# The sample's share of the input projections in float32, two column halves side by side

## The chip, the core and the metric

The kernel runs on one core of one Trainium2 chip. The metric is the device time of one execution in microseconds. Of the kernel before there are three timed runs, and one execution was taken by the hardware profiler.

## What is computed

The reference runs two layers of an encoder for 256 prompt tokens (two tiles of 128) and 64 sample tokens (one tile), with shared weights. All arrays are float32. The part that matters here is the token mixing between the two feed-forward halves:

```python
def _token_mix(h, pos, lambda_init, w_in, w_out, g_qk, w_lambda, g_sub, kv_past, s0):
    rq, rk, rv, rg, dq, dk, dv = jnp.split(h @ w_in, split_points, axis=-1)   # w_in: 1024 x 3072
    rq, rk = rotary of both, rk scaled
    o_r, s_new = _retention(rq, rk, rv, s0)
    o_r = _rms_norm(o_r) * jax.nn.silu(rg)
    dq, dk = rotary of _rms_norm of both
    o_d = _diff_attention(dq, k_all, v_all, lam, pos, k_pos)      # sample: 512 cached keys + its own 64
    o_d = _rms_norm(o_d, g_sub) * (1.0 - lambda_init)
    mix = jnp.concatenate([o_r, o_d], axis=-1) @ w_out
    return mix, dk, dv, s_new
```

Each layer computes `h` by an RMS norm with a scale and a shift for each of the two request groups, and writes the new keys, values and retention states out.

## The kernel before

**Precision.** A product of float32 tensors is made of three matmuls in the type that the listing calls F32R: both operands are split into a high part (`w_hi`, `h_hi`, by ScalarE, `split` and `norm_heads`) and a rest (`w_lo`, `h_lo`, by VectorE), and TensorE (PE in the rows) adds hi x hi, hi x lo and lo x hi. A matmul on plain float32 operands leaves two records in the trace, one for each of its passes.

**The projections.** `in_step` (L718 on) has 12 steps a layer. A step is 512 columns of `w_in` and half of the contraction, four blocks of 128 called k; two steps (kh 0 and 1) make one column block cb of 512: DK, DQ, DVAL, RQK, RV, RG. For each k the tokens are the stationary operand (two tiles of 128, one of 64) and 512 weight columns stream past: 9 matmuls of 512 columns (L740, L741, L745), three of them for the sample's 64 tokens. Outputs go to PSUM banks 0 to 2 (3 to 5 for DQ).

**The order on TensorE** is written out by hand. `attention_at(l, q)` puts the attention's pieces between the k blocks; q counts them, 48 a layer, four a step. q 10, 12, 14, 16 turn the four tiles of the key cache (`turn_nth`, L697, which waits on `cache_landed`), q 17 to 26 turn keys and queries, q 24 to 46 hold scores, transposed probabilities and weighted values of the five attention units, q 44 and 47 the retention scores. Behind the last step stand `mix_turn`, `retention` and `out_half`.

**Weights.** Each step's 1 MB lands in `raw[s % 2]` by two DMAs that SyncE's queue (SP in the rows) issues in program order (`load`, L458). Before the load of step s may start, VectorE must have finished the split of step s - 2, since that is the last reader of the buffer. The split of step s is made while step s - 1 runs. `load_in(l, 2)`, `load_in(l, 3)`, the key cache (L526) and then `load_in(l, 4)` follow one another in the queue.

**What follows the projections.** ScalarE copies (`copy_out`) or squares the tiles, VectorE rotates (`rope`, `rope_ret`), GpSimd makes the powers (`power`) and stores keys and values. All operations on the sample's tile have 64 partitions and 512 elements. VectorE's order around the wait at q 37 is: `maxima(2)`, a split, `combine(2)`, `rope_ret(0)`, `diff_sums(0)`, `rope_ret(1)`, a split, `diff_scale(0)`; `weigh(2)` at q 37 waits for the last of them. ScalarE's `exps(3)` stands behind the copies of the turns of q 38 and q 39 in its order, and `turn_probs(3)` at q 40 waits for what VectorE makes of it (`combine(3)`).

Of the kernel before, what the change touches and what calls it, by code (L numbers as in the profile page):

```python
# [19 lines left out]
F32 = mybir.dt.float32  # L20
# [21 lines left out]
ROWS = [P, P, DEC]  # L42
TILE0 = [0, P, SEQ]
# [75 lines left out]
def shape_tables():  # L119
# [9 lines left out]
    for tile in range(3):  # L129
        pos = (np.arange(P) + (PAST if tile == 2 else tile * P)).astype(np.float32)  # L130
# [6 lines left out]
        for part, f in enumerate((1.0, DH ** -0.5)):  # L137
            o = 128 * tile + 64 * part
            t[:, T_RC + o:T_RC + o + 64] = c * f
            t[:, T_RS + o:T_RS + o + 64] = s * f  # L140
    j, i = np.arange(P)[:, None], np.arange(256)[None, :]
    for h in range(HEADS):
# [4 lines left out]
        for tile in range(3):  # L147
            last = SEQ - 1 - tile * P if tile < 2 else DEC - 1
            t[:, T_KDEC + 4 * tile + h] = np.exp(g[h] * (last - np.arange(P))) if tile < 2 else \
                np.where(np.arange(P) < DEC, np.exp(g[h] * (last - np.minimum(np.arange(P), DEC - 1))), 0)  # L150
# [12 lines left out]
def encoder(nc, x_prompt, x_sample, cache_k, cache_v, state_ret, c_prompt, c_sample, w_ada, b_ada, g_norm,  # L163
# [17 lines left out]
    with ExitStack() as ctx:  # L181
# [49 lines left out]
        gsub_rows = nc.alloc_sbuf_tensor_at("gsub_rows", [P, P], F32, offset=at_rows + 3072)  # L231
        first_raw = [nc.alloc_sbuf_tensor_at(f"first_raw{s}", [P, 1024], F32, offset=at + 12288 + 4096 * s)
# [91 lines left out]
        rqk_copied = sem("rqk_copied")  # L324
        ret_first = sem("ret_first")
# [65 lines left out]

        def mix_blocks(m):
            t = MIX_ORDER[m][0]
            if MIX_ORDER[m] != (2, 1):
                return ps[:, MIX_BANK[m], :].rearrange("p (b r) -> p b r", b=4)[:, :, 0:ROWS[t]]
            return ps[:, MIX_BANK[m], 0:4 * DEC].rearrange("p (b r) -> p b r", b=4)
# [40 lines left out]
        def _(sp):  # L437
# [10 lines left out]
            def load(l, s, j, parts):  # L448
# [7 lines left out]
                wait_apart(sp, lo_ready, 4 * nn + 2 * (s % 2) + 2)  # L456
                for dst, src in parts:
# [85 lines left out]
        def _(pe):  # L543
# [146 lines left out]
            def turn(l, n, src, rows):  # L690
# [5 lines left out]
                for b in range(4):  # L696
                    mm = pe.transpose(ps[:, turn_bank(n), b * P:b * P + rows], src[0:rows, b * P:(b + 1) * P],  # L697
                                      ident[0:rows, 0:rows])
# [16 lines left out]

            def in_step(l, i, between):
# [7 lines left out]
                for hf in range(2):  # L724
                    for kk in range(2):
                        between(4 * i + 2 * hf + kk)
                        if kk == 0:
                            half_ready(l, s, 0, hf)
# [3 lines left out]
                        outs = [(ps[0:ROWS[t], first + t, :], slice(TILE0[t], TILE0[t] + ROWS[t])) for t in range(3)]  # L732
                        if cb == 0:
                            pe.wait_ge(hh_ready, l * 3 * KB + KB + k + 1)
                        for t, (out, tok) in enumerate(outs):
                            if k == 0 and cb == 4:
                                wait_apart(pe, rqk_copied, l * 3 + t + 1)
                            elif k == 0 and cb in (3, 5):
                                wait_apart(pe, copied, l * 9 + (0 if cb == 3 else 3) + t + 1)
                            pe.matmul(out, h_hi[:, k, tok], wh, start=(k == 0), stop=False)  # L740
                            pe.matmul(out, h_hi[:, k, tok], wl, start=False, stop=False)  # L741
                        if cb == 0:
                            pe.wait_ge(hl_ready, l * 3 * KB + KB + k + 1)
                        for out, tok in outs:
                            mm = pe.matmul(out, h_lo[:, k, tok], wh, start=False, stop=(k == KB - 1))  # L745
                mm.then_inc(step_done, 1)

# [52 lines left out]
            def weigh(l, n):  # L800
# [16 lines left out]
                else:  # L817
                    u = n - 2
                    for i in range(5):
                        w, v = (P, cache_val[i]) if i < 4 else (DEC, v_nat[:, 2, :])  # L820
                        for j, h in enumerate(heads):
                            mm = pe.matmul(ps[j * DEC:(j + 1) * DEC, bank, u * DV:(u + 1) * DV],
                                           probs_t[0:w, n % 2, i * P + j * DEC:i * P + (j + 1) * DEC],
                                           v[0:w, h * DV:(h + 1) * DV], start=(i == 0), stop=(i == 4))
# [3 lines left out]
            def ret_scores(l, a):  # L828
# [6 lines left out]
                for o, n, k0, q0, q1 in ((0, P, 0, 0, SEQ), (256, P, P, P, SEQ), (384, DEC, SEQ, SEQ, TOK)):  # L835
                    for b in range(2):
                        rows = slice(b * DH, (b + 1) * DH)
                        mm = pe.matmul(ps[0:n, SCORE_BANK + b, o:o + q1 - q0], rqk_t[rows, 2 + a, k0:k0 + n],
# [3 lines left out]
            def retention(l):  # L842
# [17 lines left out]
                def own(h):  # L860
                    return pe.matmul(ps[0:DEC, 2, h * DV:(h + 1) * DV], sa[0:DEC, h, :], rv_nat[0:DEC, 2, h * DV:(h + 1) * DV],
                                     start=True, stop=False)

                def carried(h):
                    rows = slice(h % 2 * DH, h % 2 * DH + DH)
                    return pe.matmul(ps[0:DEC, 2, h * DV:(h + 1) * DV], q_dec[rows, h // 2, :], state_in[rows, h // 2, :],
                                     start=False, stop=True)
# [977 lines left out]
```

## Time and profile before

| | |
|---|---|
| median of 3 runs | 1453.66 us (1451.62 to 1453.81) |
| the profiled execution, its own time | 1451.63 us |
| its span, first to last instruction | 1449.8 us |
| TensorE busy | 1391.1 us, 96% |
| VectorE, ScalarE, GpSimd busy | 865.4, 572.4, 399.1 us |
| DMA moved | 261.12 MB, mean 180 GB/s |
| the projection steps, layers 0 and 1 | 317.5 to 452.5 us and 1018.1 to 1153 us |

The table is read as follows: TensorE is busy nearly all the time, so most of the span is its stream, and a change to that stream counts unless something else sets the moment at which the stream may go on. In the stages of the projections there are such moments, and the rows below are taken from there. The lines of the page carry sums over the span; the timeline gives the start and length of single instructions, with the idle time before them and its releaser in brackets; the table by stretches gives busy times and the granted TensorE clock (1.00 is 2.4 GHz, 0.50 is 1.2 GHz).

### The profile page before, as it was taken

What the parts mean: (1) busy time and instruction counts of PE and PEld (TensorE: products, weight loads), DVE (VectorE), ACT (ScalarE), POOL (GpSimd) and SP (SyncE); (2) the same over time, 40 slices, a digit from 0 to 9 for tenths busy, and PEclk for the clock granted to TensorE, in tenths of its full rate; (3) what the DMA queues carried; (4) which work ended last, traced back from release to release, by engine and by line L of the source; (5) the groups of instructions that cost most, each with busy time, mean ns of one, the idle gap of its engine ahead of it and who ended that gap; (6) DMA issues with size and microseconds to landing.
All of it is one profiled execution on the core that took longest, in us unless ns stands there. A gap on an engine that the chain in (4) does not pass through costs nothing.

```text
span 1449.8 us, 23657 instructions
## 1 busy us (share of the span) xinstructions
PE 1391.1 (96%) x9537; PEld 1248.1 (86%) x9537; DVE 865.4 (60%) x1390; ACT 572.4 (39%) x972; POOL 399.1 (28%) x284
## 2 busy tenths in 40 slices
PE   4999999999989999999999999999999889999998
PEld 2899999977767999999999998999676679999997
DVE  2466555557565765556656665564776567666752
ACT  3343334234434543435334343433443544444421
POOL 1133233412101233333423323342120023333422
PEclk8899999999999999999999999999999999999999
DMA  9777787725321587776558777674442128455751
GB/s 318 249 241 244 228 265 219 225 81 194 125 68 52 159 254 225 239 224 193 145 151 255 241 225 232 191 206 156 149 152 89 59 86 257 130 146 147 188 157 40
DMA packets 322749, 261.12 MB, mean 180 GB/s; under 512 B 8193, under 2 KB 288337, under 8 KB 322513
## 3 DMA queue, kind: packets, MB, share of 16 engines
q1 hardware_dynamic: 321248, 255.15, 57.3%
q0 software_dynamic: 1392, 4.46, 0.9%
q8 instruction: 76, 1.25, 0.4%
q14 instruction: 33, 0.26, 0.1%
HBM read 255.12 MB, written 4.46 MB: 179 GB/s over the span
## 4 chain that ended last, share of the span: by engine, by line
PE 90%; DVE 4%; SPq 2%; ACT 1%; issue 1%; DVEq 1%; DMA 1%; ACTq 0%; POOL 0%
PE ps L573 23%; PE ps L575 22%; PE ps L574 22%; PE ps L740 4%; PE ps L599 4%; PE ps L741 4%; PE ps L745 4%; DVE w_lo L1282 1%; SPq L479 1%; SPq L458 1%; PE ps L697 1%; PE ps L652 1%; PE ps L651 1%; PE ps L656 1%; PE ps L765 1%
## 5 line engine op out<-in xcount | busy, mean ns | idle before, releaser
L1282 DVE TENSOR_TENSOR w_lo<-raw,w_hi 128x1024 fp32r<-128x1024 f32 (+3 forms) x304 | 475.3, 1605 | 68.7 <-ACT w_hi L1012 67.4
L573 PE MATMUL ps<-h_hi,w_hi 128*128 128x322 f32 x1344 | 423.2, 315 | 0.0
L575 PE MATMUL ps<-h_hi,w_lo 128*128 128x322 f32 x1344 | 417.6, 311 | 0.0
L574 PE MATMUL ps<-h_lo,w_hi 128*128 128x322 f32 x1344 | 416.6, 310 | 0.0
L1012 ACT ACTIVATE w_hi<-raw 128x1024 fp32r<-128x1024 f32 (+1 forms) x304 | 324.1, 1114 | 224.7 <-PE ps L575 184.4
L1751 POOL TENSOR_TENSOR w_lo<-raw,w_hi 128x512 fp32r<-128x512 f32 (+1 forms) x112 | 209.2, 1868 | 643.3 <-ACT w_hi L1012 643.3
L573 PEld LDWEIGHTS ps<-h_hi,w_hi 128*128 128x128 f32 x1344 | 253.2, 188 | 24.0 <-issue 24.0
L574 PEld LDWEIGHTS ps<-h_lo,w_hi 128*128 128x128 f32 x1344 | 254.3, 189 | 0.0
L575 PEld LDWEIGHTS ps<-h_hi,w_lo 128*128 128x128 f32 x1344 | 252.6, 188 | 0.0
L1077 ACT ACTIVATE t_buf<-t_buf,shift_w 128x256 f32<-128x256 f32 (+1 forms) x176 | 65.9, 421 | 415.1 <-DVE t_buf L1356 415.1
L573 PE MATMUL ps<-g_hi,w_hi 128*128 128x320 f32 x704 | 218.0, 310 | 0.0
L575 PE MATMUL ps<-g_hi,w_lo 128*128 128x320 f32 x704 | 217.4, 309 | 0.0
L574 PE MATMUL ps<-g_lo,w_hi 128*128 128x320 f32 x704 | 217.4, 309 | 0.0
L1355 DVE COPY shift_w<-ps 128x4 f32<-128x4 f32 x88 | 14.2, 161 | 202.0 <-PE ps L575 194.2
L573 PEld LDWEIGHTS ps<-g_hi,w_hi 128*128 128x128 f32 x704 | 132.4, 188 | 1.3 <-issue 1.3
L574 PEld LDWEIGHTS ps<-g_lo,w_hi 128*128 128x128 f32 x704 | 132.4, 188 | 0.0
L575 PEld LDWEIGHTS ps<-g_hi,w_lo 128*128 128x128 f32 x704 | 132.4, 188 | 0.0
L740 PE MATMUL ps<-w_hi,h_hi 128*128 128x512 f32 (+1 forms) x288 | 122.0, 424 | 6.9 <-ACT h_hi L1051 6.9
L741 PE MATMUL ps<-w_lo,h_hi 128*128 128x512 f32 (+1 forms) x288 | 116.7, 405 | 0.0
L1756 POOL TENSOR_TENSOR g_lo<-f_buf,g_hi 128x320 fp32r<-128x320 f32 x88 | 113.6, 1291 | 0.0
L1788 POOL TENSOR_TENSOR small<-small,minus_half 128x8 f32<-128x8 f32 (+4 forms) x24 | 31.1, 1299 | 283.4 <-DVE small L1442 150.4
L1371 DVE SCALAR_TENSOR_TENSOR x<-ps,mod,x 128x256 f32<-128x256 f32 x96 | 31.6, 377 | 126.5 <-PE ps L575 126.5
(173 smaller groups left out, 1470.9 us busy)
## 6 DMA issues: line engine op xcount, KB each, us to landing
raw<-in_w_ff_up SPq DMA_DIRECT2D x176, 512.0 KB, 5.1
ada_raw<-in_w_ada SPq DMA_DIRECT2D x134, 512.0 KB, 6.6
raw<-in_w_ff_down SPq DMA_DIRECT2D x64, 704.0 KB, 6.3
raw<-in_w_in SPq DMA_DIRECT2D x48, 512.0 KB, 4.8
raw<-in_w_out SPq DMA_DIRECT2D x16, 512.0 KB, 3.9
first_raw<-in_w_ada SPq DMA_DIRECT2D x10, 512.0 KB, 8.2
out<-arena POOLq DMA_DIRECT2D x9, 256.0 KB, 3.3
arena<-in_cache_k SPq DMA_DIRECT2D x2, 1024.0 KB, 7.3
```

Source lines behind the costliest of these rows:

```text
L573: pe.matmul(out, hi, mhi, start=start, stop=False)
L574: pe.matmul(out, hi, mlo, start=False, stop=False)
L575: return pe.matmul(out, lo, mhi, start=False, stop=stop)
L599: mm = pe.matmul(ps[32 * j:32 * j + 2, 4 + group % 2, 0:256], groups_c[:, :, k], ada_slot(n)[:, 256 * j:256 * j + 256], start=(k == 0), st ...
L740: pe.matmul(out, h_hi[:, k, tok], wh, start=(k == 0), stop=False)
L741: pe.matmul(out, h_hi[:, k, tok], wl, start=False, stop=False)
L745: mm = pe.matmul(out, h_lo[:, k, tok], wh, start=False, stop=(k == KB - 1))
L1012: act.activation(w_hi[s % 2][:, hf * w:(hf + 1) * w], raw[s % 2][:, hf * w:(hf + 1) * w], ACT.Copy).then_inc(hi_ready, 1)
L1077: last = act.activation(t_buf[:, s % 2, a:b], t_buf[:, s % 2, a:b], ACT.Silu, bias=shift_w[:, s % 2, 0, g:g + 1])
L1282: dve.tensor_tensor(w_lo[s % 2][:, cols], raw[s % 2][:, cols], w_hi[s % 2][:, cols], ALU.subtract)\
L1751: pool.tensor_tensor(w_lo[s % 2][:, cols], raw[s % 2][:, cols], w_hi[s % 2][:, cols], ALU.subtract)\
L1756: pool.tensor_tensor(block_of(g_lo, i + 2 * j), f_buf[:, i % 2, :], block_of(g_hi, i + 2 * j), ALU.subtract)\
```

## The change

The sample's three matmuls for each k are replaced by a float32 product from the landed weights. `in_sample` multiplies `h_sample` (64 tokens, float32, written by ScalarE instead of the sample's columns of `h_hi`) with `raw`: columns 0 to 255 into PSUM partitions 0 to 63, columns 256 to 511 into partitions 64 to 127. The call stands ahead of the step's own matmuls, behind them for cb 0. The sample's tensors behind the projections then have 128 partitions and 256 columns (`COLS`), heads 0 and 1 in the lower half, 2 and 3 in the upper; copies, squares, rotations, powers, turns, retention and stores follow that. A load must now wait until `in_sample` of the step two before has read the buffer (`sample_done`). `copy_out` takes the sample first. In `retention` the sample's matmuls have a new order with one self-wait for three. The sample's keys and values go out by two DMAs each instead of one.

```diff
@@ load
                 wait_apart(sp, lo_ready, 4 * nn + 2 * (s % 2) + 2)
+                if S_IN + 2 <= s < S_OUT + 2:
+                    wait_apart(sp, sample_done, l * IN + s - 2 - S_IN + 1)
@@ new
+            def in_sample(l, i):
+                s, cb, kh = S_IN + i, i // 2, i % 2
+                nn = l * (STEPS // 2) + s // 2
+                if cb == 0:
+                    wait_apart(pe, hh_ready, l * 3 * KB + KB + 4 * kh + 4)
+                if cb == 4 and kh == 0:
+                    wait_apart(pe, rqk_copied, l * 3 + 1)
+                elif cb in (3, 5) and kh == 0:
+                    wait_apart(pe, copied, l * 9 + (0 if cb == 3 else 3) + 1)
+                wait_apart(pe, raw_landed[s % 2], 32 * nn + 32)
+                for k in range(4):
+                    for a in range(2):
+                        o = k // 2 * W_STD + k % 2 * 512 + 256 * a
+                        mm = pe.matmul(ps[a * DEC:(a + 1) * DEC, 5 if cb == 1 else 2, 0:256], h_sample[:, 4 * kh + k, :],
+                                       raw[s % 2][:, o:o + 256], start=(kh == 0 and k == 0), stop=(kh == 1 and k == 3))
+                mm.then_inc(sample_done, 1)
@@ in_step
                         between(4 * i + 2 * hf + kk)
+                        if cb and hf == 0 and kk == 0:
+                            in_sample(l, i)
...
-                        for t, (out, tok) in enumerate(outs):
+                        for t in range(2):
...
                 mm.then_inc(step_done, 1)
+                if cb == 0:
+                    in_sample(l, i)
@@ retention
-                for h in (0, 2):
-                    own(h)
-                    carried(h)
-                own(1).then_inc(ret_first, 1)
-                wait_apart(pe, ret_first, l * 3 + 1)
-                carried(1).then_inc(ret_first, 1)
-                wait_apart(pe, ret_first, l * 3 + 2)
-                own(3).then_inc(ret_first, 1)
-                wait_apart(pe, ret_first, l * 3 + 3)
-                carried(3).then_inc(ret_done, 1)
+                own(0, True)
+                carried(0, False)
+                own(1, True)
+                sample_state(0)
+                sample_state(1)
+                carried(2, True).then_inc(ret_first, 1)
+                wait_apart(pe, ret_first, l + 1)
+                carried(1, False)
+                own(2, False)
+                own(3, True)
+                carried(3, False).then_inc(ret_done, 1)
+                sample_state(2)
+                sample_state(3)
@@ norm_heads
-                        last = act.activation(h_hi[:, kb, a:b], f_buf[:, kb % 2, a:b], ACT.Identity,
-                                              bias=mod_col(g, 1, 0, kb))
+                        last = act.activation((h_hi[:, kb, 0:SEQ], h_sample[:, kb, :])[g], f_buf[:, kb % 2, a:b],
+                                              ACT.Identity, bias=mod_col(g, 1, 0, kb))
@@ copy_out
-                    act.wait_ge(step_done, l * STEPS + S_IN + i + 3)
-                    for t in range(3):
-                        act.activation(dst[0:ROWS[t], t, :], ps[0:ROWS[t], t, :], func).then_inc(done, 1)
+                    for t in (2, 0, 1):
+                        if t == 2:
+                            act.wait_ge(sample_done, l * IN + i + 1)
+                        elif t == 0:
+                            act.wait_ge(step_done, l * STEPS + S_IN + i + 3)
+                        act.activation(dst[:, t, 0:COLS[t]], ps[:, t, 0:COLS[t]], func).then_inc(done, 1)
```

## Rows read from the trace of the kernel before

**Rows 1.** The page: busy time by engine, share of the span, instructions.
```profile
PE 1391.1 (96%) x9537; PEld 1248.1 (86%) x9537; DVE 865.4 (60%) x1390; ACT 572.4 (39%) x972; POOL 399.1 (28%) x284
```

**Rows 2.** Groups by form: stationary, moving shape, count, busy us, mean ns; first of three.
```profile
L740 PE MATMUL ps<-w_hi,h_hi 128*64 128x512 f32 x96 | 38.9, 405 | 0.0
```

**Rows 3.** Timeline of TensorE, start and length in us: one k block.
```profile
391.21 0.40 PE L740 MATMUL ps<-w_hi,h_hi 128*128 128x512 f32 x1
...
393.32 0.40 PE L740 MATMUL ps<-w_hi,h_hi 128*128 128x512 f32 x1
```

**Rows 4.** Timeline of TensorE: the sample's weighted values (two halves), then whole-array ones.
```profile
431.07 0.85 PE L745 MATMUL ps<-w_hi,h_lo 128*128 128x512 f32 x3
431.86 1.09 PE L822 MATMUL ps<-cache_val,probs_t 128*64 128x128 f32 x16
432.88 0.44 PE L822 MATMUL ps<-arena,probs_t 64*64 64x128 f32 x4
433.25 0.50 PE L740 MATMUL ps<-w_hi,h_hi 128*128 128x512 f32 x1
433.58 0.39 PE L741 MATMUL ps<-w_lo,h_hi 128*128 128x512 f32 x1
...
446.15 1.06 PE L815 MATMUL ps<-arena,probs_t 128*128 128x128 f32 x8
446.96 0.48 PE L740 MATMUL ps<-w_hi,h_hi 128*128 128x512 f32 x1
```

**Rows 5.** Timeline of TensorE: a modulation pair, float32, four side by side.
```profile
66.47 1.05 PE L599 MATMUL ps<-ada_raw,silu_c 128*2 128x256 f32 x16
67.45 0.42 PE L573 MATMUL ps<-h_hi,w_hi 128*128 128x322 f32 x1
```

**Rows 6.** Groups by form, weight loads: the loads of the first block of rows 4.
```profile
L822 PEld LDWEIGHTS ps<-cache_val,probs_t 128*64 128x64 f32 x64 | 3.8, 145 | 5.8 <-issue 5.8
```

**Rows 7.** Timeline of SyncE's queue, layer 0, and the key cache's line: issue to landing.
```profile
323.41 0.88 SPq L458 DMA_DIRECT2D raw<-in_w_in  x2
...
324.41 0.40 SPq L526 DMA_DIRECT2D arena<-in_cache_k  x1
...
DMA to landing us min/median/max: 7.0/7.3/7.6
```

**Rows 8.** Timeline of TensorE, layer 0, steps 0 to 2: q 0, q 8, q 10.
```profile
317.55 0.57 PE L740 MATMUL ps<-w_hi,h_hi 128*128 128x512 f32 x1 [3.46 <-ACT h_hi L1051]
...
336.36 0.40 PE L740 MATMUL ps<-w_hi,h_hi 128*128 128x512 f32 x1
...
340.52 0.60 PE L697 MATMUL ps<-tab,arena 128*128 128x128 f32 x4
```

**Rows 9.** Timeline of TensorE: q 32, then the waits at q 37 and q 40, both layers.
```profile
395.42 0.60 PE L795 MATMUL ps<-tab,arena 128*128 128x128 f32 x4
...
412.89 1.57 PE L822 MATMUL ps<-cache_val,probs_t 128*64 128x128 f32 x16 [2.02 <-DVE arena L1599]
427.82 0.63 PE L795 MATMUL ps<-tab,arena 128*128 128x128 f32 x4 [2.60 <-DVE arena L1643]
1114.73 1.09 PE L822 MATMUL ps<-cache_val,probs_t 128*64 128x128 f32 x16 [2.01 <-DVE arena L1599]
1128.25 0.63 PE L795 MATMUL ps<-tab,arena 128*128 128x128 f32 x4 [2.58 <-DVE arena L1643]
```

**Rows 10.** Table by stretches: busy us by engine, then PEclk, DMA share, GB/s.
```profile
317.50:321.00 3.50, 3.45 (x9) 2.38 (x10) 3.22 (x11) 1.99 (x6) 0.00 (x0) 0.54 0.00 0
415.00:418.00 3.00, 2.84 (x15) 2.04 (x12) 1.87 (x6) 0.00 (x0) 0.00 (x0) 0.50 0.35 121
```

**Rows 11.** Timeline behind step 11: the wait for the gate copies, the sample's retention.
```profile
454.55 1.13 PE L850 MATMUL ps<-arena 128*128 128x128 f32 x8 [1.19 <-issue]
...
457.40 0.43 PE L861 MATMUL ps<-arena 64*64 64x128 f32 x2
...
460.28 0.45 PE L882 MATMUL ps<-arena,k_dec 128*64 128x128 f32 x4
```

More of the change, by code:

```diff
@@ L390, in block_of, with halves, mix_dst @@
             return a[:, i, :] if isinstance(i, int) else a[:, bass.ds(i, 1), :].rearrange("p a b -> p (a b)")
+        def halves(blocks):
+            return blocks[:, :, SEQ:TOK].rearrange("p (a b) r -> p b a r", a=2)
         def mix_blocks(m):
[L393 to L396, printed above, removed]
+            t, half = MIX_ORDER[m]
+            if t < 2:
+                return ps[:, MIX_BANK[m], :].rearrange("p (b r) -> p b r", b=4)
+            if half == 1:
+                return ps[:, MIX_BANK[m], 0:4 * DEC].rearrange("p (b r) -> p b r", b=4)
+            return ps[:, MIX_BANK[m], 0:4 * DEC].rearrange("p (b a r) -> p b a r", b=2, a=2)
+        def mix_dst(m, buf):
+            t, half = MIX_ORDER[m]
+            blocks = buf[:, 4 * half:4 * half + 4, :]
+            return halves(blocks) if (t, half) == (2, 0) else blocks[:, :, TILE0[t]:TILE0[t] + ROWS[t]]
         DIFF_TILES, DIFF_BANK = (1, 2, 0), (6, 6, 7)
@@ L695, in turn @@
                     wait_apart(pe, mod_taken, FFN_GROUPS[l, 0][-1] + 1)
-                for b in range(4):
-                    mm = pe.transpose(ps[:, turn_bank(n), b * P:b * P + rows], src[0:rows, b * P:(b + 1) * P],
-                                      ident[0:rows, 0:rows])
+                for b in range(4 if rows == P else 2):
+                    mm = pe.transpose(ps[:, turn_bank(n), b * P:(b + 1) * P], src[:, b * P:(b + 1) * P], ident)
                 mm.then_inc(turned, 1)
@@ L834, in ret_scores @@
                     wait_apart(pe, ret_decayed, l * 2 + 1)
[L835 removed]
+                for o, keys, k0, q0, q1 in ((0, slice(0, P), 0, 0, SEQ), (256, slice(0, P), P, P, SEQ),
+                                            (384, slice(a * DEC, (a + 1) * DEC), SEQ, SEQ, TOK)):
                     for b in range(2):
                         rows = slice(b * DH, (b + 1) * DH)
[L838 removed]
+                        mm = pe.matmul(ps[keys, SCORE_BANK + b, o:o + q1 - q0],
+                                       rqk_t[rows, 2 + a, k0:k0 + keys.stop - keys.start],
                                        rqk_t[rows, a, q0:q1], start=True, stop=True)
@@ L869, in retention, with own @@
-                for h in (0, 2):
-                    own(h)
-                    carried(h)
-                own(1).then_inc(ret_first, 1)
-                wait_apart(pe, ret_first, l * 3 + 1)
-                carried(1).then_inc(ret_first, 1)
-                wait_apart(pe, ret_first, l * 3 + 2)
-                own(3).then_inc(ret_first, 1)
-                wait_apart(pe, ret_first, l * 3 + 3)
-                carried(3).then_inc(ret_done, 1)
+                def own(h, start):
+                    a, hv = h // 2, slice(h % 2 * DV, (h % 2 + 1) * DV)
+                    rows = slice(a * DEC, (a + 1) * DEC)
+                    return pe.matmul(ps[rows, 2, hv], sa[rows, h, :], rv_nat[rows, 2, hv], start=start, stop=not start)
@@ new lines, in carried, with sample_state @@
+                def carried(h, start):
+                    a, hv = h // 2, slice(h % 2 * DV, (h % 2 + 1) * DV)
+                    rows = slice(h % 2 * DH, h % 2 * DH + DH)
+                    return pe.matmul(ps[a * DEC:(a + 1) * DEC, 2, hv], q_dec[rows, a, :], state_in[rows, a, :],
+                                     start=start, stop=not start)
+                def sample_state(h):
+                    a, hd = h // 2, slice(h * DH, (h + 1) * DH)
+                    rows, toks = slice(h % 2 * DH, h % 2 * DH + DH), slice(a * DEC, (a + 1) * DEC)
+                    return pe.matmul(ps[rows, 3, 256 + a * DV:256 + (a + 1) * DV], k_dec[toks, 2, hd],
+                                     rv_nat[toks, 2, h % 2 * DV:(h % 2 + 1) * DV], start=True, stop=True)
@@ L893, in mix_turn @@
                 t, half = MIX_ORDER[m]
-                for b in range(4 if (t, half) != (2, 1) else 2):
-                    if (t, half) != (2, 1):
-                        src, rows = (gate_nat, q_nat)[half][0:ROWS[t], t, b * P:(b + 1) * P], ROWS[t]
-                    else:
-                        src, rows = q_nat[:, 2, b * P:(b + 1) * P], P
-                    mm = pe.transpose(ps[:, MIX_BANK[m], b * P:b * P + rows], src, ident[0:rows, 0:rows])
+                for b in range(4 if t < 2 else 2):
+                    mm = pe.transpose(ps[:, MIX_BANK[m], b * P:(b + 1) * P], (gate_nat, q_nat)[half][:, t, b * P:(b + 1) * P],
+                                      ident)
                 mm.then_inc(mix_turned, 1)
```

166 lines of the change are left out of this document (86 added, 80 removed).

## Prediction, made before the change was run

> **What bounds the kernel now.** I read the page's busy times first: TensorE is busy for 96% of the span, VectorE for 60% [rows 1]. So time on its stream is time of the kernel, unless the stream has to wait for something else soon after. The second view is the groups by form: the sample's share of the projections is three lines of 96 matmuls, 512 columns each, with 64 stationary columns [rows 2]; they cost as much as those with 128, as the length goes with the columns that stream. The third is the timeline of the two stretches of projections, for the real distance between instructions (lengths in the rows overlap) and for the waits: at the start for the norm [rows 8], at q 37 and q 40 for VectorE [rows 9], behind the last step [rows 11]. Last the clock: after the norm's wait, and after that at q 37, the granted clock is 0.54 and 0.50, the 1.2 GHz level [rows 10]; behind the longer wait at q 40 the three matmuls at 431.07 have the distance of the 2.4 GHz level [rows 4].
>
> **What is removed.** One k block takes 393.32 - 391.21 = 2.11 us for 9 matmuls, 0.234 us each [rows 3]. Three of nine go: 0.70 us a k, 2.81 us a step, 67.5 us over 24 steps.
>
> **What is added.** A block of 8 float32 matmuls per step, 256 columns, two by two on the two column halves. The nearest row is the sample's weighted values: 16 records are 8 matmuls of 128 columns with the same 128*64 stationary, two by two, and they take 432.88 - 431.86 = 1.02 us [rows 4]; with twice the columns that is 2.04 us. The modulation pair has the column count: 16 records are 8 matmuls of 256 columns, four side by side, 67.45 - 66.47 = 0.98 us for two k [rows 5]; two k of mine would take the same if it is the column that costs, so 1.96 us for four. Float32 on the whole array: 4 matmuls of 128 columns in 446.96 - 446.15 = 0.81 us [rows 4], so 0.20 us for 128 columns and 0.40 us for 256; four such lengths, perfect pairs, are 1.6 us, and eight, no pairing, 3.2 us. To each comes the change between kinds of matmul: 0.09 us at the entry (431.86 less 431.07 and three times 0.234) and 0.10 us at the exit (433.58 - 433.25 - 0.234) [rows 4]. So 1.8 to 3.4 us, and I take 2.1, near the block that has the same stationary shape. Net: 0.7 us a step; if all of it counted, 24 x 0.7 = 17 us.
>
> The tiling page of the Trainium skill (TensorEngine Tiling (Array Packing), Key Properties) says that a change of tiling mode drains the engine. The entry and exit rows have that change in them, at 0.1 us a side; were each drain as long as a matmul outlasts its distance (0.39 - 0.23 us), the 48 changes would cost 7.7 us instead of 4.6, and the sum 3 us less.
>
> **What does not count, stage by stage (one layer).**
>
> Steps 0 and 1. The block stands behind the step here, and the load of step s + 2 now waits for it; the key cache is queued behind the load of step 3. Before, that load was issued at 323.41 and the cache at 324.41, and it landed 7.0 to 7.6 us later [rows 7], ahead of q 10 at 340.52 [rows 8]. After, eight k blocks lose 5.6 us and two sample blocks add 4.2, so q 8 moves from 336.36 to 334.9. The load of step 3 is issued there, the cache at 335.9, landing at 342.9 to 343.5. TensorE is at q 10 at 334.9 + 2.1 + 2 x 1.41 = 339.8. It waits some 3.4 us: a new wait in place of a gain, and q 10 comes 2.4 to 3.0 us later than now; I take 2.7. Queued behind the waiting turn is the whole stream of TensorE; SP holds load 4 behind the cache, which it needs two steps later. Step 2's weights are loaded from the end of step 0 on, and step 1 and two sample blocks lie over that load and its split. ScalarE's split for step 3 comes as late as its load and holds the squares of the keys back, by as much as q 10 is late (2.7 us); six k blocks and more, 12 us, lie between q 10 and the first turn of a key at q 17, so that hides; without that cover it would cost those 2.7 us.
>
> q 10 to q 32. Two k blocks (1.4) and five steps (3.5): 4.9 us gained. No wait of 0.7 us or more stands there now, and a step loses only 0.7 us of about ten, so I take it that none appears; the bound, one such wait a step, is 3.5 us.
>
> q 32 to q 37. The wait at q 37 ends when VectorE has done its queue, which starts with the scores at q 32, and the change takes nothing from that queue: `rope_ret(2)` comes later. q 37 stays 412.89 - 395.42 = 17.5 us behind q 32 [rows 9]. TensorE arrives 0.7 us earlier by step 8, 0.7 by q 36 and 2.1 later by the block of step 9, so the wait shrinks from 2.0 to about 1.3 us and nothing is gained.
>
> q 37 to q 40. `exps(3)` waits for the turn of q 39, so the two k blocks before that turn count (1.4 us); the one behind it lengthens the wait from 2.6 to some 3.3 us.
>
> Steps 10 and 11: 2 x 0.7 = 1.4 us.
>
> Behind them. `retention` waits 1.19 us for three gate copies [rows 11], of which the sample's is done earlier (some 0.5 us). The sample's eight retention matmuls take 460.28 - 457.40 = 2.9 us [rows 11]; with one self-wait for three I take 0.7 us off (0 to 1.5). 1.2 us together. VectorE, ScalarE and GpSimd work less on the sample (half the elements for each partition); it counts only in these waits. Two more stores on GpSimd's queue have the powers of the attention behind them, due at q 37 at the earliest, more than 17 us later: nothing.
>
> Sum: +2.7 - 4.9 - 1.4 - 1.4 - 1.2 = -6.2 us a layer, -12.4 us for both.
>
> **The clock.** The norm's wait of 3.46 us is followed by the low level, the 2.6 us at q 40 is not [rows 4, 8 to 10]. A new wait of 3.4 us resembles the first; 3.4 us at half clock cost 1.7 us. I count that once for each cache wait (+3.4), set what a longer wait at q 40 risks against what the shorter one at q 37 spares, and leave it there: in layer 0 q 37 to q 40 took 14.93 us and in layer 1 13.52 [rows 9], so one low stretch more or less is worth 1.4 us there. -12.4 + 3.4 = -9 us.
>
> The profiled execution took 1451.6 us, which gives 1442.6; the median of the runs lies 2.0 us above it, which gives 1444.7. I forecast 1444 us.
>
> **Rivals.** (1) The cache wait and the clock cost little: the transfer lands early, since less is in flight than before, and q 37 keeps the clock up. Then the sum is -12.4 with most of the two delays of 2.7 us taken out, or -17: 1437 us. For it: the transfer alone moves 1 MB; against it: the same two transfers stood one behind the other in the row that gave 7.0 us.
> (2) The gain is swallowed: the block costs 2.5 us instead of 2.1, or the low clock follows all four waits. 24 x 0.4 x 0.8 (the share of the steps that counts) = 8 us less: 1452 us, no change.
> (3) Slower: the two halves do not run side by side, the block takes 3.2 + 0.2 = 3.4 us against 2.81 removed. Place: every step; it decides from some 2.4 us up, where the gain of the counting steps no longer pays for the delay at q 10. Price: 24 x 0.6 = 14 us lost, with 5.4 + 3.4 us of waits and clock, less 2.4 behind the steps: +20 us, 1474 us. This is also the case in which the change does not do what its words say. For it: both halves use the same 128 rows, and each matmul has two loads and two passes in order. Against it: the weighted values have both properties and took 1.02 us where eight unpaired lengths are 1.6 us [rows 4].
> TensorE: Matmul & The Clock Gate, in the Trainium skill (Part 3, The mechanism), says that a weight load overlaps running matmuls only where its row group differs, which here it never does; by that rule 16 loads add to the block and rival 3 would be right. The 64 loads of the nearest row have a mean of 145 ns and 59 ns of busy time each [rows 6]: 16 in a row would be 2.3 us, more than the whole block of 1.02 us, so the trace disagrees.
>
> **How the numbers follow.** Forecast 0.50, its own range 1439 to 1449; rival 1 0.22; rival 2 0.18; rival 3 0.10. The range must leave out no more than 2 in 10: rival 3 and the edges of the others, 1434 to 1454. A measurement of this kernel tells 0.2% (2.9 us) from no change. Faster than 1450.8: forecast nearly whole (0.48), rival 1, and a third of rival 2 (0.06): 0.76. Same: half of rival 2 and a bit of the forecast: 0.12. Slower: rival 3 and the tail of rival 2: 0.12.
>
> **What would show it.** In the profile after: two lines of 128*64 float32 matmuls from `raw`, blocks of some 2.1 us, 24 of them; no sample forms on the three lines of `in_step`; k blocks of 1.41 us; a wait of 3 to 4 us at the first cache turn, ended by the DMA; q 37 17.5 us behind q 32 as before; the wait at q 40 longer than 2.6 us. Wrong if the blocks take 2.5 us or more, if the first turn does not wait, or if a wait appears in steps 3 to 7.

## The result, and the profile after

The changed kernel takes 1434.26 us (median, 1432.1 to 1435.38); the kernel before, run beside it, 1453.18 us. The ratio is 0.9868, 95% interval 0.9857 to 0.9880: 18.9 us faster, twice the 9 us forecast. The profiled execution took 1433.75 us, 17.9 less than the one of before.

The page of after: busy time by engine, share of the span, instructions (answers rows 1).

```profile
PE 1363.1 (95%) x9617; PEld 1231.0 (86%) x9617; DVE 854.9 (60%) x1366; ACT 570.3 (40%) x972; POOL 397.9 (28%) x288
```

Groups by form of after: the sample's product (answers rows 2).

```profile
L751 PE MATMUL ps<-raw,h_sample 128*64 128x256 f32 x384 | 48.1, 393 | 3.6 <-DVEq L1713 3.6
```

Timeline of TensorE, after, layer 0: k blocks and one sample block (answers rows 3 and 4).

```profile
344.91 0.39 PE L781 MATMUL ps<-w_hi,h_hi 128*128 128x512 f32 x1
...
346.30 0.60 PE L718 MATMUL ps<-tab,arena 128*128 128x128 f32 x4
346.82 1.95 PE L751 MATMUL ps<-raw,h_sample 128*64 128x256 f32 x16
348.70 0.50 PE L781 MATMUL ps<-w_hi,h_hi 128*128 128x512 f32 x1
349.04 0.40 PE L782 MATMUL ps<-w_lo,h_hi 128*128 128x512 f32 x1
```

A k block is 346.30 - 344.91 = 1.39 us (forecast 1.41). The sample's block is 348.70 - 346.82 = 1.88 us, and its exit costs 349.04 - 348.70 - 0.234 = 0.11 us: 2.0 us without its entry (forecast 2.1 with an entry of 0.09). Over 24 blocks the group gives 48.1 us. The price of the edit was right.

Timeline of TensorE, after, layer 0: the instructions in front of which it was idle, in brackets the wait and what ended it (answers rows 8, 9 and 11; layer 1 has the same waits within 0.2 us).

```profile
316.38 0.76 PE L781 MATMUL ps<-w_hi,h_hi 128*128 128x512 f32 x1 [3.46 <-ACT h_sample L1101]
...
336.63 1.95 PE L751 MATMUL ps<-raw,h_sample 128*64 128x256 f32 x16 [1.74 <-DVEq L1713]
...
343.01 0.66 PE L718 MATMUL ps<-tab,arena 128*128 128x128 f32 x4 [1.45 <-DMA arena<-in_cache_k]
...
361.81 0.63 PE L718 MATMUL ps<-tab,arena 128*128 128x128 f32 x4 [1.10 <-ACT arena L1176]
...
410.16 1.09 PE L867 MATMUL ps<-cache_val,probs_t 128*64 128x128 f32 x16 [1.61 <-DVE arena L1657]
420.79 0.63 PE L839 MATMUL ps<-tab,arena 128*128 128x128 f32 x4 [3.29 <-DVE arena L1701]
434.37 1.19 PE L884 MATMUL ps<-arena 64*128 64x256 f32 x12 [0.75 <-ACT arena L1196]
447.21 1.13 PE L897 MATMUL ps<-arena 128*128 128x128 f32 x8 [0.72 <-issue]
```

New are the waits at the start of step 2 (336.63), at the cache (343.01) and at 434.37. The wait at q 18 (361.81) grew from 0.61 to 1.10 us; in the kernel before its row is:

```profile
360.17 0.63 PE L697 MATMUL ps<-tab,arena 128*128 128x128 f32 x4 [0.61 <-ACT arena L1123]
```

The wait at q 37 shrank from 2.02 to 1.61 us, the one at q 40 grew from 2.60 to 3.29 us.

Table by stretches of after: behind q 37, behind q 40 (answers rows 10; the column behind the engines is PEclk).

```profile
410.00:414.00 4.00, 3.68 (x38) 3.04 (x39) 1.60 (x5) 0.00 (x0) 0.00 (x0) 1.00 0.37 144
420.80:424.00 3.20, 3.20 (x25) 2.58 (x27) 0.43 (x1) 2.39 (x4) 0.00 (x0) 0.59 0.02 5
```

The low level has moved. Before, it stood behind q 37 and not behind q 40 [rows 4, 10]; now it stands behind q 40 and not behind q 37.

From the same timelines, us from one place to the next. "To the retention" ends with the retention's first matmul, "end" with the first matmul of the next stage.

```
                q0 to q10  to q32  to q37  to q40  to the retention   end    sum
before  layer 0     22.97   54.90   17.47   14.93             26.73   9.55  146.55
        layer 1     24.26   54.88   17.46   13.52             26.73  11.09  147.94
after   layer 0     26.63   49.72   17.43   10.63             26.42   8.40  139.23
        layer 1     26.51   49.65   17.41   10.61             26.49   8.39  139.06
change  layer 0     +3.66   -5.18   -0.04   -4.30             -0.31  -1.15   -7.32
        layer 1     +2.25   -5.23   -0.05   -2.91             -0.24  -2.70   -8.88
forecast, each      +4.4    -4.9     0      -1.4              -1.9   -0.7    -4.5
```

(The forecast's +4.4 is 2.7 and the clock's 1.7; its 0.5 for the gate copies stands ahead of the retention.) The two layers give 16.2 us. The remaining 1.7 us of the profiled difference lie outside: 1.2 us ahead of the projections of layer 0 (317.55 to 316.38), where the kernels run below scatter from 314.5 to 318.0 us, and 0.5 us behind them.

### The profile page after: what moved, and what is told of

Same layout as the page of the kernel before. It is cut to its first block, busy times and chain, and to the rows that moved or that the text cites. A ratio compares the mean times of both kernels' runs of the same rounds, so it can differ in the third digit from the quotient of the medians.

```text
span 1431.9 us, 23847 instructions
## 1 busy us (share of the span) xinstructions
PE 1363.1 (95%) x9617; PEld 1231.0 (86%) x9617; DVE 854.9 (60%) x1366; ACT 570.3 (40%) x972; POOL 397.9 (28%) x288
## 4 chain that ended last, share of the span: by engine, by line
PE 87%; DVE 5%; SPq 2%; ACT 2%; DMA 1%; DVEq 1%; issue 1%; POOL 0%; ACTq 0%
PE ps L594 23%; PE ps L596 22%; PE ps L595 22%; PE ps L620 4%; PE ps L781 2%; PE ps L782 2%; PE ps L786 2%; DVE w_lo L1339 2%; PE ps L751 2%; SPq L500 1%; SPq L479 1%; PE ps L809 1%; DMA raw<-in_w_in 1%; PE ps L673 1%; PE ps L672 1%
## 5 line engine op out<-in xcount | busy, mean ns | idle before, releaser
L1127 ACT ACTIVATE t_buf<-t_buf,shift_w 128x256 f32<-128x256 f32 (+1 forms) x176 | 65.9, 421 | 414.2 <-DVE t_buf L1411 414.2
L1845 POOL TENSOR_TENSOR small<-small,minus_half 128x4 f32<-128x4 f32 (+2 forms) x24 | 27.9, 1169 | 273.1 <-DVE small L1497 149.0
L781 PE MATMUL ps<-w_hi,h_hi 128*128 128x512 f32 x192 | 83.3, 434 | 6.9 <-ACT h_sample L1101 6.9
L1416 DVE SCALAR_TENSOR_TENSOR f_buf<-f_buf,shift_w,t_buf 128x256 f32<-128x256 f32 (+1 forms) x176 | 60.0, 382 | 36.8 <-ACT t_buf L1127 36.8
```

Source lines behind the costliest of these rows:

```text
L781: pe.matmul(ps[:, first + t, :], tok, wh, start=(k == 0), stop=False)
L1127: last = act.activation(t_buf[:, s % 2, a:b], t_buf[:, s % 2, a:b], ACT.Silu, bias=shift_w[:, s % 2, 0, g:g + 1])
L1416: last = dve.scalar_tensor_tensor(f_buf[:, u, a:b], f_buf[:, u, a:b], shift_w[:, u, 1, g:g + 1], t_buf[:, u, a:b], ALU.add, ALU.mult)
```

## The experiments

Diffs are against the kernel after unless said otherwise. Theory A (C in e5 and e6) is mine in each. The milestones are those of the table above.

**The halves side by side.** `e4_unpaired` sends both column halves to the same partitions, so its sample columns are not the reference's.

```diff
-    mm = pe.matmul(ps[a * DEC:(a + 1) * DEC, 5 if cb == 1 else 2, 0:256], h_sample[:, 4 * kh + k, :],
-                   raw[s % 2][:, o:o + 256], start=(kh == 0 and k == 0), stop=(kh == 1 and k == 3))
+    mm = pe.matmul(ps[0:DEC, 5 if cb == 1 else 2, 0:256], h_sample[:, 4 * kh + k, :],
+                   raw[s % 2][:, o:o + 256], start=(kh == 0 and k + a == 0), stop=(kh == 1 and k + a == 4))
```

> The changed kernel with both column halves of the sample's product sent to the same PSUM partitions, so that they use the same column half of the array and nothing is side by side (the sample's values are left wrong by that, the work after them is the same). Theory A (the halves overlap in the changed kernel): the block of 16 records goes from 2.0 us to 3.2 to 3.6 us, 24 blocks add 29 to 38 us, of which the stretch from q 32 to q 37 gives some back to the wait there: 25 to 34 us more than the changed kernel, 1459 to 1468 us, slower than the kernel before. Rival B (the halves do not overlap, and the block is cheap for another reason): the block stays at 2.0 us and the time at 1434 us.

It took 1466.18 us, ratio to before 1.0091 (1.0076 to 1.0107): 32 us more than after. Timeline of TensorE, a block of it:

```profile
360.74 3.67 PE L751 MATMUL ps<-raw,h_sample 128*64 128x256 f32 x16
```

Groups by form: the same kernel's matmuls, then the weight loads of after.

```profile
L751 PE MATMUL ps<-raw,h_sample 128*64 128x256 f32 x384 | 89.7, 387 | 0.2 <-issue 0.2
```

```profile
L751 PEld LDWEIGHTS ps<-raw,h_sample 128*64 128x64 f32 x384 | 26.9, 140 | 21.4 <-issue 11.8
```

3.67 us where the paired block has 1.95, 89.7 us in all where it has 48.1. The loads and the columns are the same, only the place of the output differs: the halves run side by side. In e4 all eight matmuls also add up in one place, which this run does not separate from the column half; but eight lengths of the whole-array row, unpaired, are 3.2 us [rows 4], so no second cause is needed for most of the 1.7 us between the two blocks. This is rival 3 of the prediction, and it is slower than before, as that rival said. The paired block also decides against the sentence of the Trainium skill that the prediction cites (TensorE: Matmul & The Clock Gate, Part 3, The mechanism): its 16 loads use the same 128 rows and take 140 ns each in the mean, 2.2 us together, and yet the whole block takes 1.88 us.

**The two new waits ahead of q 10.** `e1_cache_first` issues the key cache ahead of the loads of steps 2 and 3; `e2_banks_first` lets VectorE report the free banks before its split for step 2; `e3_both_first` does both.

```diff
@@ e1, e3: SyncE
-                for i in (2, 3):
-                    load_in(l, i)
-
                 ...
                 sp.dma_start(scratch, ck_d[l]).then_inc(cache_landed, 16)
+                for i in (2, 3):
+                    load_in(l, i)
@@ e2, e3: VectorE
-                split(l, S_IN + 2)
                 take(FFN_GROUPS[l, 0][-1])
                 dve.drain().then_inc(banks_free, 1)
+                split(l, S_IN + 2)
                 split(l, S_IN + 3)
```

> The changed kernel with one move: the load of the key cache stands ahead of the loads of steps 2 and 3 in SyncE's queue. Theory A (the two new waits stand one behind the other and both count): the wait at q 10 (1.45 and 1.26 us in the two layers) goes, the one at the start of step 2 (1.74 and 1.83 us) stays or grows by what the cache takes from the load of step 2; 2.5 us less than the changed kernel, some 1431.8 us. Rival B (what is saved here is lost at the next wait, at q 17 to 19, as VectorE's rotation is late): no difference, 1434.3 us.

> The changed kernel with one move: VectorE frees the banks of step 2 ahead of the split for step 2 instead of behind it. Theory A: the wait at the start of step 2 (1.74 and 1.83 us) goes, but the key cache lands when it lands, so the wait at q 10 grows by as much, to some 3.2 us; no difference in time, 1434.3 us, and if the low clock follows the longer wait, up to 3.4 us more. Rival B (the waits are independent): 3.5 us less, 1430.8 us.

> Both moves together. Theory A: neither wait is left, 3.2 and 3.1 us less in the two layers, 6 us less than the changed kernel, some 1428 us. Rival B (VectorE's rotation or the split for step 2 ends next): 2.5 us or less is gained, 1431.8 us or more.

All three end at the time of after: 1433.48 (ratio to before 0.9871, 0.9856 to 0.9886), 1434.63 (0.9879, 0.9864 to 0.9893) and 1434.35 us (0.9881, 0.9861 to 0.9901). My theory held for e2 alone. Timeline of TensorE, the waits up to q 18 of e1, then of e2, then of e3:

```profile
336.21 1.95 PE L751 MATMUL ps<-raw,h_sample 128*64 128x256 f32 x16 [1.74 <-DVEq L1713]
...
361.14 0.63 PE L718 MATMUL ps<-tab,arena 128*128 128x128 f32 x4 [2.23 <-ACT arena L1176]
```

```profile
341.79 0.66 PE L718 MATMUL ps<-tab,arena 128*128 128x128 f32 x4 [3.40 <-DMA arena<-in_cache_k]
```

```profile
353.10 0.63 PE L718 MATMUL ps<-tab,arena 128*128 128x128 f32 x4 [2.20 <-DVEq L1563]
...
361.25 0.63 PE L718 MATMUL ps<-tab,arena 128*128 128x128 f32 x4 [0.62 <-ACT arena L1176]
```

What one wait loses, the next one gains. The time to q 28 is 66.3 us in layer 0 of after (26.63 + 39.69) and 65.9, 64.8 and 64.7 us here. But the 1.5 us and more by which e2 and e3 lead there arise ahead of the waits that were moved: up to q 8 (here the start of the sample's block of step 1) after takes 16.56 us in layer 0, e2 and e3 15.20 and 15.12 with the same matmuls, and the granted clock in the 4 us behind the norm's wait is 0.50, 0.62 and 0.64. 1.25 us go again behind q 40, where their stretch to the retention takes 27.7 us instead of 26.4. From q 8 to q 28, in us:

```
layer 0 / layer 1     q8 to q28
after               49.76 / 49.59
e1_cache_first      49.51 / 49.42
e2_banks_first      49.64 / 49.58
e3_both_first       49.62 / 49.58
e9_rope_only        48.89 / 48.50
e8_rope_early       45.38 / 44.92
```

So the waits of step 2, of the cache and of q 18 are not three costs but one chain: step 2's and step 3's weights are loaded late, hence split late, and VectorE's split for step 3 stands ahead of its rotation of the keys.

**That chain.** `e8_rope_early` is e3 with the rotation taken out of it: ScalarE's key squares come ahead of its split for step 3, VectorE's split comes behind the first rotated key tile. `e9_rope_only` has this part without the two moves of e3.

```diff
@@ ScalarE
-                    split(l, S_IN + i + 2)
+                    if i != 1:
+                        split(l, S_IN + i + 2)
                     ...  (the squares of the keys)
+                    if i == 1:
+                        split(l, S_IN + 3)
@@ VectorE, natural rotation
                         dve.tensor_tensor(d, d, na, ALU.add).then_inc(nat_ready, 1)
+                        if i == 1 and j == 0:
+                            split(l, S_IN + 3)
@@ VectorE, start
-                split(l, S_IN + 3)
                 rope(1)
```

> The kernel with both moves at the start (cache ahead, banks freed ahead), and the squares of the keys on ScalarE ahead of its split for step 3, VectorE's part of that split behind the first rotated tile. Theory A (with both moves made, the wait of 2.2 us at q 16 and the one at q 18 come from the rotation of the keys, which stands behind the split of a load that comes late): both waits go and 2 to 2.8 us a layer are gained, 1429 to 1430.5 us. Rival B (the split for step 3 itself ends last): no difference to the changed kernel, 1434 us, or a new wait at step 3.

> The kernel after with one part of e8_rope_early alone: the key squares of step 1 stand on ScalarE ahead of its split for step 3, and VectorE's split for step 3 stands behind the first rotated key tile. The cache issue and the banks_free of step 2 stay where the kernel after has them. Theory A (one chain: each of the three parts of e8 is needed, since a wait taken from one place only goes to the next): the waits of step 2 (1.7 to 1.8 us) and of the cache (1.3 to 1.5 us) stay, the one at q18 (1.10 us) goes or shrinks; 1 to 1.5 us per layer, 1431 to 1432.5. Rival B (the rotation order was the bound by itself, and the two early waits only filled time that the rotation would have taken): most of the gain of e8_rope_early comes with this part alone, 1422.5 to 1426.

e8 takes 1422.59 us (ratio to before 0.9804, 0.9790 to 0.9818), e9 1432.48 us (0.9864, 0.9845 to 0.9884). In e8 one wait over 0.2 us is left in each layer between the first matmul of the projections and q 37, of 0.37 us at q 18 in layer 0 and of 0.43 us in step 0 of layer 1, and q 0 to q 28 takes 60.6 and 59.4 us instead of 66.3 and 66.1. All three moves give 11.7 us, more than twice what I expected. Of that 1.4 and 2.0 us in the two layers stand ahead of q 8, where e8's granted clock behind the norm's wait is 0.62 and 1.00; the chain itself is worth 4.4 and 4.7 us from q 8 to q 28, the rotation order alone 0.9 and 1.1, the two moves alone 0.1 and 0.0. The chain needs all its links cut.

**How much of the removed work counts.** `e7_no_sample` is the kernel before without the sample's matmuls (one is left for each column block, 12 in all, to define its output); `e11_half_block` is the kernel after with two of the four k in each sample block.

```diff
@@ e7, against before
-                            pe.matmul(out, h_hi[:, k, tok], wh, start=(k == 0), stop=False)
-                            pe.matmul(out, h_hi[:, k, tok], wl, start=False, stop=False)
+                            if t < 2 or k == 0:
+                                pe.matmul(out, h_hi[:, k, tok], wh, start=(k == 0), stop=(t == 2))
+                            if t < 2:
+                                pe.matmul(out, h_hi[:, k, tok], wl, start=False, stop=False)
...
-                        for out, tok in outs:
+                        for out, tok in outs[:2]:
@@ e11
-                for k in range(4):
+                for k in range(2):
                 ...  (the end of the accumulation likewise)
```

> The kernel before with the sample's matmuls in the projections left out, but for one in every 24 or so (one per column block, 12 of 288; the sample's values are wrong by that, all work behind them is done). What the removal alone is worth: 276 x 0.234 = 64.6 us if TensorE's stream were all that counts. Theory A (q 32 to q 37 belongs to VectorE and gives nothing, and from q 17 to q 28 its rotation ends next in part): 48 to 56 us less than the kernel before, 1398 to 1406 us, so that the 24 blocks of 2.0 us cost 28 to 36 us of their 48. Rival B (everything counts): 64 us less, 1389 us.

> The kernel after with every block of the sample halved: 2 of its 4 k blocks, so half of the sample's part of the projections is left out. A block then costs 1.0 us instead of 2.0, over 24 steps 24 us of TensorE's work less. Theory A (TensorE's work is what bounds the steps, up to a point where the other engines' splits take over; e7_no_sample, with 48 us less, gained 20): the first half is worth more than the second, 13 to 18 us less than after, 1416 to 1421, with a wait at q18 of 2 to 3 us. Rival B (each microsecond taken is worth the same share, 0.42): 10 us, 1424.

e7 takes 1414.16 us (0.9739, 0.9725 to 0.9752), 38.4 less than before; both theories asked for more. Timeline of TensorE in e7: the waits at q 18 and q 37.

```profile
354.57 1.09 PE L697 MATMUL ps<-tab,arena 128*128 128x128 f32 x4 [4.13 <-ACT arena L1125]
...
400.37 1.98 PE L824 MATMUL ps<-cache_val,probs_t 128*64 128x128 f32 x16 [5.17 <-DVE arena L1601]
```

e11 takes 1427.74 us (0.9834, 0.9818 to 0.9850), 6.5 less than after (4.9 by the two ratios to before), and misses both: the first 24 us taken off the blocks give 5 to 6.5, the other 24 some 14. The smaller share goes with waits and clock: its wait at step 2 is 2.78 and 2.70 us, at q 18 2.80 and 1.51 us, at q 37 3.35 us, and behind q 37 the low level follows, so that q 37 to q 40 takes 13.6 us in both layers instead of 10.6. Because of that, e11 does not price a sample block cleanly, and the two points don't give a law. Nor does e7: it has the sample's layout and the retention of the kernel before (9.55 us to the end where after has 8.40), and the low level behind q 18 and q 37 (0.50 in the 4 us behind each, in both layers). The 20 us between it and after (1434.3 - 1414.2), of the 48 us which 24 blocks cost, are what two different kernels show and not the price of the blocks.

**The clock.** Each of these kernels fills waits of TensorE with float32 matmuls of 128 columns that nothing reads: `e5_before_busy37` (kernel before) the one at q 37, `e6_after_busy40` the one at q 40, `e10_both_busy` (e8) those at q 40 and of the norm, `e12_three_busy` that of q 37 as well.

```diff
+            def keep_busy(count, bank):
+                for _ in range(count):
+                    pe.matmul(ps[:, bank, 384:512], ones[:], ident, start=True, stop=True)
@@ weigh (e5: 9, e12: 7)
+                    keep_busy(7, 7)
                     wait_apart(pe, diff_out, l * 3 + 1)
@@ turn_probs (e6, e10, e12)
+                if n == 3:
+                    keep_busy(14, 6)
                 wait_apart(pe, p_ready, l * NU + n + 1)
@@ ahead of in_step (e10, e12)
+                keep_busy(15, 3)
```

> The kernel before, with nine float32 matmuls of 128 columns (some 1.8 us) put into TensorE's wait of 2.0 us at q 37; their result is read by nobody. Theory C (what q 37 to q 40 gained in the changed kernel beyond its two k blocks is the granted clock, which fell after the wait of 2.0 us before and does not after the one of 1.6 us now): q 37 to q 40 falls from 14.93 and 13.52 us to some 12.0 us (the 10.6 us of the changed kernel and two k blocks of 0.7 us), 4.4 us in all, 1449 us. Rival D (the gain there is VectorE's shorter work on the sample): the stretch stays above 13 us, 1453 us.

> The changed kernel with fourteen float32 matmuls of 128 columns (some 2.8 us) in the wait of 3.3 us at q 40. Theory C (steps 10 and 11 give back their gain, since the granted clock falls after that wait): q 40 to the retention falls from 26.4 us to 24.7 to 25.3 us, 2 to 3 us in all, 1431 to 1432 us. Rival D (ScalarE's and VectorE's chain of the last attention unit sets that stretch): it stays at 26.4 us, 1434 us.

> e8_rope_early with TensorE kept busy in its two longest waits by matmuls of a matrix of ones that nothing reads: 14 float32 matmuls of 128 columns while it waits for the norm of q (q40, 3.3 us) and 15 in the wait of the hidden state's norm ahead of the projections (3.46 us). Theory A (the low granted clock behind these two waits is caused by the idle stretch itself): q40 gives 1.5 us per layer as in e6_after_busy40, the norm's wait 1 to 3 us per layer from a low stretch of 3.4 to 6.8 us behind it; 1413 to 1418. Rival B (behind the norm the work is bound by the splits and not by TensorE's clock, so a higher clock there only lengthens the next wait): only the 3 us of q40, 1419 to 1420.

> e10_both_busy with a third wait filled: 7 more float32 matmuls of 128 columns that nothing reads, in the 1.5 to 1.6 us before the weighting with the cached values (q37), behind which e10 ran at a granted clock of 0.72 to 0.86 and took 12.2 us for q37 to q40 instead of 10.6. Theory A (each low stretch hangs on its own wait, and a low stretch that is spared elsewhere can come at a wait that had gone without): q37 to q40 falls to 10.6 in both layers, 3.1 us less than e10_both_busy, about 1417. Rival B (the low level only moves on again, to the next wait behind q40, as it moved from q40 to q37): q40 to the retention, or the retention to the end of the layer, grows by 1.5 us per layer, about 1420.

Between the milestones, in us:

```
layer 0 / layer 1       q0 to q28     q37 to q40    q40 to retention    retention to end
e5_before_busy37     66.87 / 66.87  12.00 / 12.00    26.73 / 26.75       11.09 /  9.55
after                66.32 / 66.13  10.63 / 10.61    26.42 / 26.49        8.40 /  8.39
e6_after_busy40      66.33 / 66.82  10.64 / 12.16    24.89 / 24.89        8.40 /  8.39
e8_rope_early        60.58 / 59.44  10.62 / 10.59    26.42 / 26.42        8.39 /  8.39
e10_both_busy        59.44 / 59.44  12.18 / 12.16    24.89 / 24.91        8.39 /  8.39
e12_three_busy       59.46 / 59.44  10.68 / 10.64    24.91 / 24.89        8.39 /  8.40
```

e5: 1446.96 us, 0.9965 (0.9952 to 0.9977); e6: 1431.46, 0.9857 (0.9843 to 0.9870); e10: 1419.99, 0.9779 (0.9761 to 0.9797); e12: 1417.66, 0.9752 (0.9739 to 0.9766). Tables by stretches behind q 37 and behind q 40, of e10, then of e12:

```profile
404.00:408.00 4.00, 3.84 (x33) 3.05 (x30) 2.00 (x6) 0.00 (x0) 0.00 (x0) 0.72 0.29 110
415.90:419.00 3.10, 3.07 (x33) 2.39 (x35) 0.30 (x1) 2.26 (x4) 0.00 (x0) 1.00 0.00 0
```

```profile
404.00:408.00 4.00, 3.84 (x40) 3.11 (x37) 1.97 (x6) 0.08 (x1) 0.00 (x0) 1.00 0.32 123
415.90:419.00 3.10, 3.10 (x28) 2.01 (x25) 1.78 (x2) 2.21 (x3) 0.00 (x0) 1.00 0.02 5
```

A filled wait is followed by the high level each time: q 37 gives 2.9 and 1.5 us in e5, q 40 1.5 and 1.6 us in e6. But the low level can then stand at a wait that had gone without it. In layer 1 of e6 q 37 to q 40 takes 1.55 us more than in after, and q 8 to q 28, with the low level behind the cache, 1.9 us more (51.46); in e10 q 40 gives 1.5 and q 37 takes 1.55, so of e10's expected 3 us there nothing is left. That the filling moves the level there is not shown: e9, which fills nothing, has it at q 37 of layer 1 too, where q 37 to q 40 takes 12.15 us. Its row of the table by stretches:

```profile
1101.31:1105.31 4.00, 3.84 (x33) 3.10 (x34) 1.74 (x5) 0.00 (x0) 0.00 (x0) 0.74 0.36 137
```

The norm's wait gives 1.1 us in layer 0 of e10 and nothing in layer 1, where e8 had the high level behind that wait already. With q 37 filled too (e12), q 37 to q 40 is back at 10.6 us, the granted clock is 1.00 behind every wait of both layers' projections, and the two layers are 3.0 us shorter than in e10, as A said; the medians differ by 2.3 us. e12 beats both kernels: 2.5% under before, 16.6 us under after.

## Why the prediction was right in the sign and wrong in the size

**Right.** The k block and the sample's block (1.39 and 2.0 us for 1.41 and 2.1); halves side by side (e4); q 10 to q 32 at -5.2 (forecast -4.9), though the claim that no wait of 0.7 us appears there was wrong: 0.61 us at q 18 became 1.10; q 32 to q 37 unchanged, since VectorE's queue sets it; the wait at q 40 at 3.29 us (3.3); q 10 later by 3.7 and 2.3 us (2.7 without the clock). With the halves in one place e4 lost 32 us to after; rival 3 had 30 between itself and the forecast.

**Wrong: "I count that once for each cache wait (+3.4)".** No low level follows the cache wait in after: in the 4 us behind it the granted clock is 1.00 in both layers. The wait is only 1.45 us there, as 1.74 us of the delay already stand in the wait of step 2. In e2 the whole 3.40 us stand at the cache, as forecast to a tenth, and still the level stays high; this row of e2's table by stretches begins with the wait's end:

```profile
342.00:346.00 4.00, 4.00 (x24) 3.18 (x24) 2.82 (x7) 1.54 (x3) 2.63 (x2) 1.00 0.43 159
```

So the length of the norm's 3.46 us, from which the term was taken, does not carry over to another wait. (That a low level can come at the cache is shown by layer 1 of e6, with 0.65 behind 2.53 us.) The stage as a whole came 2.9 us under the forecast, for both layers together: the 3.4 us did not come, and the delay was 0.5 us more than 2 x 2.7 (5.9). In it stands the clock behind the norm's wait, which differs between executions: up to q 8 the kernel before takes 18.81 us in layer 0 (granted clock 0.57 in the first 4 us) and 20.09 in layer 1 (0.50), where after has 0.50 in both layers. Layer 1, with the same level in both kernels, gives the delay as 2.25 us, layer 0 as 3.66.

**Wrong: "set what a longer wait at q 40 risks against what the shorter one at q 37 spares, and leave it there".** I left the two clock risks at zero. Measured, the stage q 37 to q 40 gained 4.30 and 2.91 us for a forecast 1.4: 4.4 us for both layers come from the level that stays at 2.4 GHz behind q 37, as e5 shows on the kernel before, where filling that wait alone takes q 37 to q 40 from 14.93 and 13.52 to 12.00 us; less the 1.4 us forecast that is the 10.6 of after. It is in part luck that both layers of after have it: layer 1 of e6 and of e9, whose waits at q 37 are as long (1.61 and 1.62 us), have the low level there and take 12.16 and 12.15 us. At q 40 the other risk did come true: the low level followed the longer wait, and the 1.9 us forecast for the stage became 0.3. In e6, with that wait filled, the stage takes 24.89 us, where the forecast meant 26.73 - 1.9 = 24.8: the clock is nearly the whole of the loss, 3.1 of 3.25 us over both layers. The gain at q 37 is the larger of the two, and I had put neither into the sum.

**Wrong in size: "I take 0.7 us off (0 to 1.5)" for the sample's retention.** The stretch to the end lost 1.15 us in layer 0. The further 1.5 us of layer 1 are no gain of the change's own work: before has a low stretch there (granted clock 0.85 over 11.09 us, against 1.00 over 9.55 in layer 0), and e5 has it in the other layer (0.85 over 11.09, 1.00 over 9.55).

**Wrong: two covers.** "step 1 and two sample blocks lie over that load and its split" and "lie between q 10 and the first turn of a key at q 17, so that hides". Neither did: the wait of step 2 is VectorE's split for the late load, behind which the report of free banks is queued (in e2, with the report ahead of the split, it is gone); and the late rotation shows at q 18, whose wait is gone in e9. That they cost nothing in the sum of the stages is luck of a kind: they stand in series with the cache wait, so the sum of them came out as the one delay I had forecast. e1 to e3 show that, and e8 that the chain is worth 4.4 and 4.7 us in the two layers.

Added up over both layers against the forecast: -2.9 (start), -0.6 and -0.1 (up to q 37), -4.4 (q 37), +3.25 (q 40), -2.45 (the retention's end) make -7.2, the difference of 9.0 and 16.2; 1.7 us more lie outside the layers. Rival 1 named the half that came true ("q 37 keeps the clock up"); its other half, that the transfer lands early, did not: the cache was issued at 336.00 and TensorE's turn began at 343.01, 7.0 us, as before [rows 7]. Rival 1's 1437 us lies nearest to the result, but by another sum: the delays at q 10 stood (5.9 us in all), and the clock at q 37 gave 4.4 us back. Timeline of SyncE's queue, after, the cache's issue:

```profile
336.00 0.39 SPq L547 DMA_DIRECT2D arena<-in_cache_k  x1
```

## What to carry to other kernels

When a load is moved later, follow its whole chain (load, split, what stands behind the split on each engine) to the last consumer. If several waits hang on one chain, a move that takes one away only feeds the next, and the worth shows only when all links are cut (here, from q 8 to q 28 of both layers, at most 0.4 us for the moves at the start, 2.0 for the rotation order and 9.0 for all). Put each wait's clock into the sum as a term with both its values, also where a wait gets shorter; and look for a wait that had gone without the low level before counting on what a filled one gives.

## What the runs showed of the hardware

The low level did not go by the length of the wait alone. The granted clock in the 4 us behind a wait: behind the norm's 3.46 us it is 0.50 to 0.64 in every layer that left it empty but one, 1.00 in layer 1 of e8; behind 2.20 us at q 16 0.66 (e3); behind 3.40 us at the cache 1.00 (e2), behind 2.53 us there 0.65 (e6, layer 1); behind 2.60 us at q 40 1.00 (before), behind 3.29 us 0.50 to 0.61 (after, e1, e2, e3, e8); behind 2.0 us at q 37 0.56 and 0.72 (before), behind 1.5 to 1.6 us 1.00 (after), but 0.74 and 0.75 in e10 and 0.74 in layer 1 of e6 and of e9. Filling a wait with work was followed by the high level behind it every time, and sometimes by the low one at a wait that had gone without; but e9 has that too, with no wait filled. What picks the waits is left open.
